# Transposes of a convolution's columns moved from the matmul engine to DMA, in a hybrid decoder block on one Trainium2 core

## The chip, the cores and the metric

The kernel runs on one core of one Trainium2 chip. The metric is the device time of the core in microseconds (us), the median of three runs. One further execution was taken with the hardware profiler, and all rows below come from it. The engines are PE (TensorE, matmuls; its weight loads are listed as PEld), DVE (VectorE), ACT (ScalarE), POOL (GpSimd) and SP (SyncE, which here only issues DMA transfers).

## What is computed

One layer of a decoder block on x of 256 tokens by 2048, all in float32:

```
hn = RMSNorm(h)
[q | k | v | z | xBC | dt | gate] = hn @ w_in
attention: per head, RMSNorm of q and k, ALiBi, causal (256 tokens are one MoBA block)
ssm: xBC = silu(causal depthwise conv over 4 tokens of xBC + bias)
     xs, B, C = split(xBC)              # 4096, 1024, 1024 columns
     y = chunked SSD scan(xs, dt, a, B, C), chunks of 128 tokens, 8 groups
     y = (y + d_skip * xs) * silu(z), RMSNorm per group of 512 columns, times norm_w
h += (sigmoid(g1) * (attn @ w_attn_out) + sigmoid(g2) * (y @ w_ssm_out)) @ w_out
h += relu(RMSNorm(h) @ w_up)^2 @ w_down
```

The projection xBC has 6144 columns: B and C (2048) are wanted with channels on the partitions, xs (4096) with tokens on the partitions. The convolution runs over tokens, so it is done with channels on the partitions, where a shift by a token is a shift in the free dimension.

## The kernel before

All large products go through one stream of **blocks**, numbered 0 to 87. A block is 512 columns of one weight matrix times 2048 rows, in 8 **units** of two 128-row tiles. SP loads a unit into one of four raw slots (`load_block`, L366), ACT rounds it to whi (L849), DVE takes the rest, wlo = raw - whi (L1268), and PE does three matmuls per tile and token half: xh*whi, xh*wlo, xl*whi (L485 to L487), 12 per unit and 96 per block, into two PSUM banks of a set (`stream`, L469). ACT and DVE work `LEAD` = 3 units ahead of PE: in step s of a block their program has the split of unit s+3 and then the other work put at step s (`steps`, L851 and L1271). There is no scheduler: every engine runs its program in the written order, and a wait holds up all that is behind it on that engine. SP loads a unit once the split four units earlier has freed the slot (L369).

Blocks 12 to 23 (`B_CONV` = 12) are the projection xBC: conv blocks m = 0 to 3 are B and C, m = 4 to 11 are xs. Conv block m is projected in block 12+m and convolved during block 13+m:

- ACT evacuates the PSUM set at step 7, scaled, to c_st (`conv_evac`, L1021).
- PE turns c_st into channel-major form in 8 transposes of 128x128 in float32, a matmul with the identity (`conv_T`, L645, recorded at L454), after unit 1, into PSUM banks 4 and 5.
- ACT makes the first tap with the bias from PSUM (`conv_first`, L1030), DVE adds three taps for each of four column tiles (`conv_taps`, L1451, 12 operations), ACT applies silu (`conv_silu`, L1043).
- For m of 4 and up, PE turns the result back in 8 transposes (`conv_back`, L662) after unit 6, and ACT copies it to xs (`conv_out`, L1049).

Conv block 11 has both of its transposes and all its taps in block 24, the first block of the SSD phase (`B_SSD` = 24). The common order of an SSD block is: PE does the product C*B (`seg`, L720) after unit 1 and the y product (`ssd_y`, L703, 8 products recorded at L710) after unit 4; DVE makes M, the decay matrix, in `ssd_seg` at step 0 (L1495, L1498), ACT takes its exponential (`ssd_exp`, L1080) at step 2, DVE multiplies it (`ssd_M`, L1515) at step 3. In block 24 these stand later: seg after unit 5, y after unit 7. POOL sets up the parameters of the next conv block (`conv_par`, L1802) once the taps of the last are done, and then the operands of the SSD groups (`ssd`, L1816): BTg, CTg, xd, xf.

The MLP's blocks already turn a tile by DMA: ACT splits r_st into its two 16-bit planes (`r_halve`, L1224), SP issues one `dma_start_transpose` per plane (`r_turn`, L359), and DVE joins the planes (`f_join`, L1676).

Of the kernel before, what the change touches and what calls it, by code (L numbers as in the profile page):

```python
# [22 lines left out]
D = 2048  # L23
T = 256
# [37 lines left out]
def build(nc, x, mix_norm_w, w_in, q_norm_w, k_norm_w, conv_w, conv_b, dt_bias, a_log, d_skip, ssm_norm_w,  # L62
# [13 lines left out]
    with ctx:  # L76
# [48 lines left out]
        c_st = [sb(f"c_st{i}", "E", 4 * KB * i, [P, NTOK, COLS]) for i in range(2)]  # L125
        cacc = sb("cacc", "E", 8 * KB, [P, 4, T])
        cT = sb("cT", "E", 12 * KB, [P, 4, T])
# [145 lines left out]

        c_T = sem("c_T")
# [83 lines left out]
        def _(sp):  # L358
# [7 lines left out]
            def load_block(b, w, row0, col0, turn=None):  # L366

                for s in range(SLOTS if isinstance(b, int) and b == 0 else 0, US):
# [4 lines left out]
                    if turn is not None and s >= US - 2:  # L373
                        r_turn(turn, s - US + 2)

# [22 lines left out]
            with sp.Fori(0, 4) as m:  # L398
                load_block(B_CONV + m, w_in, 0, XBC0 + INNER + m * COLS)
            with sp.Fori(0, 8) as m:  # L400
                load_block(B_CONV + 4 + m, w_in, 0, XBC0 + m * COLS)
# [10 lines left out]
            def ssd_loads(j1):  # L412
                load_rows(4 * j1 - 4, 2 * j1 - 2, 0)
                load_block(B_SSD + 4 * j1 - 4, w_in, 0, Z0 + 2 * j1 * COLS - 2 * COLS)
                load_rows(4 * j1 - 3, 2 * j1 - 2, 1)
                load_block(B_SSD + 4 * j1 - 3, w_in, 0, GATE0 + j1 * COLS - COLS)
# [33 lines left out]
        def _(pe):  # L450
# [194 lines left out]
            def conv_T(m, i, staged, backs):  # L645

                def f():
                    pe.wait_ge(set_free[i], staged)
                    if later(m):
                        pe.wait_ge(c_silu, m)  # L650
                        if later(backs):
                            pe.wait_ge(c_out, backs)
                    else:
                        pe.wait_ge(set_free[2], 4)
                    for c in range(4):
                        for t in range(NTOK):
                            o = (c % 2) * T + t * P
                            last = transpose(ps[4 + c // 2][:, o:o + P], c_st[i][:, t, c * P:(c + 1) * P])
                    last.then_inc(c_T, 1)
                return f  # L660

            def conv_back(m, src):  # L662
                def f():
                    pe.wait_ge(c_silu, m + 1)
                    for t in range(NTOK):
                        for c in range(4):
                            last = transpose(ps[4 + t][:, c * P:(c + 1) * P], src[:, c, t * P:(t + 1) * P])
                    last.then_inc(c_back, 1)
                return f

            a = attention(3)

            def conv_after(m, i, staged, backs, src=None, more=None):
                d = dict(more or {})
                d[1] = d.get(1, []) + [conv_T(m, i, staged, backs)]
                if src is not None:
                    d[6] = d.get(6, []) + [conv_back(m, src)]
                return d

# [3 lines left out]
            stream(B_CONV + 1, 1, 4, xT_hi, xT_lo, after=conv_after(0, 0, 5, 0, more=a[1]))  # L683
            stream(B_CONV + 2, 0, 5, xT_hi, xT_lo, after=conv_after(1, 1, 5, 0, more=a[2]))
            stream(B_CONV + 3, 1, 5, xT_hi, xT_lo, after=conv_after(2, 0, 6, 0))
            stream(B_CONV + 4, 0, 6, xT_hi, xT_lo, after=conv_after(3, 1, 6, 0))
# [3 lines left out]
            stream(B_CONV + 11, 1, 9, xT_hi, xT_lo, after=conv_after(10, 0, 10, 6, cT))  # L690
# [24 lines left out]
            def ssd_after(n, c, g):  # L715
# [9 lines left out]
                def banks_free():  # L725
                    pe.wait_ge(c_out, 8)
# [112 lines left out]
        def _(act):  # L839
# [181 lines left out]
            def conv_evac(m, k, i):  # L1021
                def f():
                    block_done(B_CONV + m)
                    if not (isinstance(m, int) and m < 2):
                        act.wait_ge(c_T, m - 1)
                    A(c_st[i][:, 0, :], SETS[k][0][:, :], ACT.Copy, scale=rstd1[:, 0:1])
                    A(c_st[i][:, 1, :], SETS[k][1][:, :], ACT.Copy, scale=rstd1[:, 1:2]).then_inc(set_free[k], 1)
                return f

            def conv_first(m):  # L1030
                def f():
                    act.wait_ge(c_T, m + 1)
                    act.wait_ge(c_par, m + 1)
                    if later(m):
                        act.wait_ge(c_silu, m)
                    for c in range(4):
                        i = A(cacc[:, c, :], ps[4 + c // 2][:, (c % 2) * T:(c % 2 + 1) * T], ACT.Identity,
                              scale=cw[:, 3, c:c + 1], bias=cb[:, c:c + 1])
                        if c % 2:
                            i.then_inc(c_first, 1)  # L1040
# [8 lines left out]
            def conv_out(m):  # L1049
# [855 lines left out]
```

## Time and profile before

| | |
|---|---|
| three runs | 2054.35, 2055.06, 2055.19 us, median 2055.06 |
| the profiled execution | 2054.75 us, its span 2052.7 us |
| granted TensorE clock | 1.0 of full speed over the whole span |
| busy, share of the span | PE 99%, PEld 83%, DVE 59%, ACT 51%, POOL 9% |
| DMA | 394 MB, 192 GB/s |

The span runs from the first to the last record of the core; the 2.05 us beside it are start and end. Conv blocks 12 to 23 lie at about 309 to 590 us, the SSD blocks 24 to 39 at 590 to 985 us, the MLP from 1353 us. "Busy" for PE means that some matmul was in flight: matmuls of 0.39 us start every 0.227 us. A bracket at the end of a timeline row gives the idle time of the engine before it and what ended it.

### The profile page before, as it was taken

To read this page: it belongs to the slowest core of one execution; us is meant where nothing else is said; L and a number is where in the kernel's file an instruction comes from. 1 tells how busy PE (TensorE), PEld (TensorE's weight loads), DVE (VectorE), ACT (ScalarE), POOL (GpSimd) and SP (SyncE) were. 2 spreads that over 40 slices of the span, in tenths; PEclk is the share of its full clock that TensorE was granted. 3 is DMA by queue.
4 is the path that set the end of the run, shared out by engine and by line. 5 is a ranking of instruction groups with operands and counts; after the bars stand their busy time and mean duration, and the time that the engine had idled before them with its cause. 6 is when DMAs were issued, how large, how long until landed. Compare 5 with 4: busy or idle time off the path is not lost.

```text
span 2052.7 us, 27154 instructions
## 1 busy us (share of the span) xinstructions
PE 2041.6 (99%) x9374; PEld 1694.7 (83%) x9374; DVE 1216.3 (59%) x1346; ACT 1037.7 (51%) x1238; POOL 189.4 (9%) x210
## 2 busy tenths in 40 slices
PE   9999999999999999999999999999999999999999
PEld 8888888888888888888888888888888888888887
DVE  5665566666666666666655555555545555554654
ACT  6454555555565454545554444455435534534542
POOL 2110010000012111111210000000000000000000
PEclk9999999999999999999999999999999999999999
DMA  7656555656665655666555556567667666666765
GB/s 241 186 164 183 166 167 171 178 176 179 178 201 177 194 194 184 196 198 190 174 183 185 193 187 225 194 185 223 203 193 211 213 193 202 204 210 194 201 218 163
DMA packets 231213, 394.08 MB, mean 192 GB/s; under 512 B 45776, under 2 KB 46736, under 8 KB 230880
## 3 DMA queue, kind: packets, MB, share of 16 engines
q1 hardware_dynamic: 229712, 389.54, 62.0%
q10 hardware_dynamic: 960, 2.75, 0.4%
q0 software_dynamic: 464, 0.77, 0.2%
q8 instruction: 47, 0.77, 0.2%
q14 instruction: 30, 0.25, 0.0%
HBM read 382.46 MB, written 2.16 MB: 187 GB/s over the span
## 4 chain that ended last, share of the span: by engine, by line
PE 97%; DVE 1%; ACT 1%; issue 0%; DMA 0%; DVEq 0%; ACTq 0%
PE ps L485 31%; PE ps L487 31%; PE ps L486 30%; PE ps L454 2%; PE ps L710 1%; ACT whi L849 0%; PE ps L562 0%; PE ps L539 0%; PE ps L699 0%; DVE f_st L1682 0%; DVE fT_lo L1690 0%; PE ps L720 0%; DVE cacc L1462 0%; ACT fT_hi L1236 0%; DVE wlo L1268 0%
## 5 line engine op out<-in xcount | busy, mean ns | idle before, releaser
L1268 DVE TENSOR_TENSOR wlo<-raw,whi 128x1024 fp32r<-128x1024 f32 x703 | 892.2, 1277 | 669.1 <-ACT whi L849 667.4
L849 ACT ACTIVATE whi<-raw 128x1024 fp32r<-128x1024 f32 x703 | 736.5, 1058 | 645.5 <-PE ps L487 628.6
L485 PE MATMUL ps<-whi,xT_hi 128*128 128x512 f32 x1276 | 509.5, 399 | 0.0
L487 PE MATMUL ps<-whi,xT_lo 128*128 128x512 f32 x1276 | 498.1, 390 | 0.0
L486 PE MATMUL ps<-wlo,xT_hi 128*128 128x512 f32 x1276 | 496.9, 389 | 0.0
L487 PEld LDWEIGHTS ps<-whi,xT_lo 128*128 128x128 f32 x1276 | 239.5, 188 | 51.3
L486 PEld LDWEIGHTS ps<-wlo,xT_hi 128*128 128x128 f32 x1276 | 240.0, 188 | 47.8 <-issue 1.0
L485 PEld LDWEIGHTS ps<-whi,xT_hi 128*128 128x128 f32 x1276 | 239.8, 188 | 47.8 <-issue 1.3
L485 PE MATMUL ps<-whi,fT_hi 128*128 128x512 f32 x512 | 199.6, 390 | 3.3 <-DVE fT_lo L1690 3.3
L485 PE MATMUL ps<-whi,hT_hi 128*128 128x512 f32 x512 | 199.3, 389 | 0.0
L487 PE MATMUL ps<-whi,fT_lo 128*128 128x512 f32 x512 | 199.2, 389 | 0.0
L486 PE MATMUL ps<-wlo,fT_hi 128*128 128x512 f32 x512 | 199.2, 389 | 0.0
L487 PE MATMUL ps<-whi,hT_lo 128*128 128x512 f32 x512 | 199.2, 389 | 0.0
L486 PE MATMUL ps<-wlo,hT_hi 128*128 128x512 f32 x512 | 199.2, 389 | 0.0
L485 PEld LDWEIGHTS ps<-whi,fT_hi 128*128 128x128 f32 x512 | 96.1, 188 | 24.8 <-ACT whi L849 3.8
L486 PEld LDWEIGHTS ps<-wlo,hT_hi 128*128 128x128 f32 x512 | 96.1, 188 | 20.0
L487 PEld LDWEIGHTS ps<-whi,hT_lo 128*128 128x128 f32 x512 | 96.1, 188 | 19.9
L487 PEld LDWEIGHTS ps<-whi,fT_lo 128*128 128x128 f32 x512 | 96.1, 188 | 19.9
L486 PEld LDWEIGHTS ps<-wlo,fT_hi 128*128 128x128 f32 x512 | 96.1, 188 | 19.9
L485 PEld LDWEIGHTS ps<-whi,hT_hi 128*128 128x128 f32 x512 | 96.1, 188 | 19.8
L485 PE MATMUL ps<-whi,sT_hi 128*128 128x512 f32 x256 | 99.9, 390 | 0.0
L487 PE MATMUL ps<-whi,sT_lo 128*128 128x512 f32 x256 | 99.6, 389 | 0.0
(254 smaller groups left out, 1856.7 us busy)
## 6 DMA issues: line engine op xcount, KB each, us to landing
raw<-in_w_in SPq DMA_DIRECT2D x319, 512.0 KB, 3.8
raw<-in_w_up SPq DMA_DIRECT2D x128, 512.0 KB, 4.1
raw<-in_w_down SPq DMA_DIRECT2D x128, 512.0 KB, 4.3
raw<-in_w_ssm_out SPq DMA_DIRECT2D x64, 512.0 KB, 4.2
raw<-in_w_attn_out SPq DMA_DIRECT2D x32, 512.0 KB, 4.3
raw<-in_w_out SPq DMA_DIRECT2D x32, 512.0 KB, 4.4
arow<-arows SPq DMA_DIRECT2D x16, 512.0 KB, 4.9
h<-in_x ACTq DMA_DIRECT2D x1, 2048.0 KB, 12.0
```

Source lines behind the costliest of these rows:

```text
L454: return nc.tensor.transpose(dst, src, ident[:, :])
L485: mm(dst, xh, whi[sl][:, kk, :], start=(s == 0 and kk == 0), stop=False)
L486: mm(dst, xh, wlo[sl][:, kk, :], start=False, stop=False)
L487: last = mm(dst, xl, whi[sl][:, kk, :], start=False, stop=(s == US - 1 and kk == UK - 1))
L710: last = mm(ps[6][:, hh * SHD:(hh + 1) * SHD], M[:, hh, :], xf[:, hh, :], start=True, stop=True)
L849: A(whi[s % SLOTS][:, :, :], raw[s % SLOTS][:, :, :], ACT.Copy).then_inc(hi_ready, 1)
L1268: V.tensor_tensor(wlo[s % SLOTS][:, :, :], raw[s % SLOTS][:, :, :], fp(whi[s % SLOTS][:, :, :]), ALU.subtract).then_inc(lo_ready, 1)
```

## The change

1. Conv blocks 0 to 10 are turned to channel-major form by DMA. ACT, which evacuates as before, splits c_st into two 16-bit planes (`c_halve`, step 0), SP turns each plane by a DMA transpose (`c_turn`: the first after the load of unit 7 of the block, the second after unit 0 of the next; SP runs about 7 units ahead of PE), and DVE joins them to cx (`c_join`, step 3). The taps read cx in SBUF instead of PSUM.
2. For m = 4 to 10 the result goes back the same way: `x_halve` on ACT (step 2 of the next block), `x_turn` on SP (after units 2 and 3), `x_join` on DVE (step 7), straight into xs.
3. Conv block 11 keeps PE's transposes, in block 24, where the SSD work takes its common place, and the taps stand around it.
4. The convolution works one half block later than before: first tap at step 4, taps at steps 5 and 6, silu at step 1 of the next block.
5. c_st has one buffer instead of two. SP's conv loop and DVE's loops are written out or shortened; POOL waits for two groups of xs before its SSD work instead of one.

```diff
+            def c_turn(m, a):
+                sp.wait_ge(c_halved, m + 1)
+                if m:
+                    sp.wait_ge(c_joined, m)
+                sp.dma_start_transpose(c_tiles[:, a, :, :], c_half[:, a, :, :].rearrange("p t n -> p (t n)")) \
+                    .then_inc(c_turned, 16)
+            def x_turn(m, a):
+                sp.wait_ge(x_halved, m - 3)
+                if m > 4:
+                    sp.wait_ge(c_out, m - 4)
...
+            def conv_turns(j, s):
+                if s == 0 and 2 <= j <= 12:
+                    c_turn(j - 2, 1)
+                if s in (2, 3) and 7 <= j <= 13:
+                    x_turn(j - 3, s - 2)
+                if s == 7 and 1 <= j <= 11:
+                    c_turn(j - 1, 0)
...
-            stream(B_CONV + 1, 1, 4, xT_hi, xT_lo, after=conv_after(0, 0, 5, 0, more=a[1]))
...
-            with pe.Fori(0, 3) as i:
-                stream(B_CONV + 5 + 2 * i, 1, 6 + i, xT_hi, xT_lo, after=conv_after(4 + 2 * i, 0, 7 + i, 2 * i, cT))
-                stream(B_CONV + 6 + 2 * i, 0, 7 + i, xT_hi, xT_lo, after=conv_after(5 + 2 * i, 1, 7 + i, 1 + 2 * i, cT))
+            stream(B_CONV + 1, 1, 4, xT_hi, xT_lo, after=a[1])
...
+            with pe.Fori(0, 4) as i:
+                stream(B_CONV + 4 + 2 * i, 0, 6 + i, xT_hi, xT_lo)
+                stream(B_CONV + 5 + 2 * i, 1, 6 + i, xT_hi, xT_lo)
...
-                return {0: [conv_T(11, 1, 10, 7)], 3: [conv_back(11, cT)], 5: [banks_free, seg],
-                        7: [ssd_y(n, c, g)]}
+                return {0: [conv_T], 1: [banks_free, seg], 4: [ssd_y(n, c, g)], 7: [conv_back]}
...
+            def c_halve(m, k, staged):
+                def f():
+                    act.wait_ge(set_free[k], staged)
+                    if later(m):
+                        act.wait_ge(c_turned, 32 * m)
+                    A(c_half[:, :, :, :].rearrange("p a t n -> p a (t n)"),
+                      halves(c_st[:, :, :].rearrange("p t n -> p (t n)")), ACT.Copy).then_inc(c_halved, 1)
...
+            def conv_work(j, k, staged, more=None):
                 d = dict(more or {})
+                add(d, 0, c_halve(j - 1, 1 - k, staged))
...
+                    add(d, 1, conv_silu(j - 2, dst))
+                    if not (isinstance(j, int) and j < 6):
+                        add(d, 2, x_halve(j - 2))
+                add(d, 4, conv_first(j - 1))
+                add(d, 7, conv_evac(j, k))
...
-                    steps(b, {1: [conv_first(11)], 3: [conv_silu(11, cT[:, :, :])], 4: [conv_out(11)],
-                              6: [ssd_exp(n)], 7: [z_sigmoid(b, g)]})
+                    steps(b, {1: [ssd_exp(n), conv_silu(10, cacc[:, :, :])], 2: [x_halve(10)], 3: [conv_first(11)],
+                              6: [conv_silu(11, cacc[:, :, :])], 7: [conv_out, z_sigmoid(b, g)]})
...
+            def c_join(m):
+                def f():
+                    dve.wait_ge(c_turned, 32 * m + 32)
+                    if later(m):
+                        dve.wait_ge(c_tap, 12 * m)
+                    for a in range(2):
+                        i = V.tensor_copy(halves(cx[:, :, :].rearrange("p c t -> p (c t)"))[:, a, :],
+                                          c_tiles[:, a, :, :].rearrange("p (t c) l -> p c t l", t=NTOK))
...
+            def conv_work(j, more=None):
                 d = dict(more or {})
+                add(d, 3, c_join(j - 1))
+                add(d, 5, conv_taps(j - 1, 0))
+                add(d, 6, conv_taps(j - 1, 1))
+                if not (isinstance(j, int) and j < 6):
+                    add(d, 7, x_join(j - 2))
...
-                    steps(b, {0: [ssd_seg(n, 0, g)], 1: [conv_taps(11, 0, 0), conv_taps(11, 0, 1)],
-                              2: [conv_taps(11, 1, 0), conv_taps(11, 1, 1)],
-                              6: [ssd_cbm(n, 0, g)], 7: [ssd_M(n), z_gate(g), ssd_y(n, 0, g)]})
+                    steps(b, {0: [ssd_seg(n, 0, g)], 1: [ssd_cbm(n, 0, g)], 3: [ssd_M(n)], 4: [conv_taps(11, 0)],
+                              5: [ssd_y(n, 0, g), conv_taps(11, 1)], 7: [z_gate(g)]})
...
-            pool.wait_ge(c_out, 1)
+            pool.wait_ge(c_out, 2)
```

On PE, in block 23 (conv block 11 is projected, 10 convolved), the end of unit 1 before:

```order
L487 MATMUL ps<-whi_54,xT_lo 128x512
L454 MATMUL ps<-ident,c_st_91 128x128 [waits c_out,c_silu,set_free0]
L454 MATMUL ps<-ident,c_st_91 128x128 x7
L485 MATMUL ps<-whi_55,xT_hi 128x512 [waits lo_ready,hi_ready]
```

Such a group, and one of cT after unit 6, is gone from each block of the loop and from this one. The c_st group that is left stands in block 24, after unit 0; now:

```order
L520 MATMUL ps<-whi_53,xT_lo 128x512
L487 MATMUL ps<-ident,c_st 128x128 [waits set_free2,set_free1]
L487 MATMUL ps<-ident,c_st 128x128 x7
L518 MATMUL ps<-whi_54,xT_hi 128x512 [waits lo_ready,hi_ready]
```

On ACT, from the split of unit 6 to M's exponential in block 24 before (L849 is the weight split, M the decay matrix):

```order
L849 ACTIVATE whi_55<-raw_51 128x1024 [waits unit_used,raw_in2]
L1046 ACTIVATE cT<-cacc 128x1024 [waits c_tap]
L849 ACTIVATE whi_56<-raw_52 128x1024 [waits unit_used,raw_in3]
L1053 ACTIVATE xs<-ps 128x512 [waits c_back]
L1054 ACTIVATE xs<-ps 128x512
L849 ACTIVATE whi_53<-raw_49 128x1024 [waits unit_used,raw_in0]
L849 ACTIVATE whi_54<-raw_50 128x1024 [waits unit_used,raw_in1]
L1083 ACT_TABLE_LOAD
L1083 ACTIVATE M<-M 128x1024 [waits seg_done]
```

and now, from the split of unit 4 to that of unit 6 and the first tap behind it (L860 is the weight split):

```order
L860 ACTIVATE whi_53<-raw_49 128x1024 [waits unit_used,raw_in0]
L1116 ACT_TABLE_LOAD
L1116 ACTIVATE M<-M 128x1024 [waits seg_done]
L1073 ACT_TABLE_LOAD
L1073 ACTIVATE cacc<-cacc 128x1024 [waits c_tap]
L860 ACTIVATE whi_54<-raw_50 128x1024 [waits unit_used,raw_in1]
L1081 ACTIVATE x_half<-cacc 128x2048 [waits x_turned,c_silu]
L860 ACTIVATE whi_55<-raw_51 128x1024 [waits unit_used,raw_in2]
L1065 ACTIVATE cacc<-ps,cb,cw 128x256 [waits c_silu,x_halved,c_par,c_T]
```

M's exponential moved from between the splits of units 9 and 10 to just behind that of unit 4, and silu and x_halve of conv block 10 stand between it and the splits of units 5 and 6.

On DVE, around M's product in block 24 now (L1303 is the weight split, L1569 the product that y waits for):

```order
L1303 TENSOR_TENSOR wlo_58<-raw_50,whi_54 128x1024 [waits hi_ready]
L1303 TENSOR_TENSOR wlo_59<-raw_51,whi_55 128x1024 [waits hi_ready]
L1569 TENSOR_TENSOR M<-M,cbm 128x1024 [waits dec_done,cbm_done]
L1303 TENSOR_TENSOR wlo_60<-raw_52,whi_56 128x1024 [waits hi_ready]
L1510 SCALAR_TENSOR_TENSOR cacc<-ps,cw,cacc 128x255 [waits c_first]
```

Before, all taps of conv block 11 stood ahead of that product; now it stands behind the split of unit 6 alone, and they behind it.

## Rows read from the trace of the kernel before

**Rows 1.** The page: span, busy time, chain of waits, the weight split of ACT, raw's landing.

```profile
span 2052.7 us, 27154 instructions
...
PE 2041.6 (99%) x9374; PEld 1694.7 (83%) x9374; DVE 1216.3 (59%) x1346; ACT 1037.7 (51%) x1238; POOL 189.4 (9%) x210
...
PE 97%; DVE 1%; ACT 1%; issue 0%; DMA 0%; DVEq 0%; ACTq 0%
...
L849 ACT ACTIVATE whi<-raw 128x1024 fp32r<-128x1024 f32 x703 | 736.5, 1058 | 645.5 <-PE ps L487 628.6
...
raw<-in_w_in SPq DMA_DIRECT2D x319, 512.0 KB, 3.8
```

**Rows 2.** PE's groups by line: matmul or transpose, busy us, mean ns, idle before.

```profile
L485 PE MATMUL ps<-whi,fT_hi 128*128 128x512 f32 x512 | 199.6, 390 | 3.3 <-DVE fT_lo L1690 3.3
...
L454 PE MATMUL ps<-ident,c_st 128*128 128x128 f32 x96 | 12.4, 272 | 0.0
...
L454 PE MATMUL ps<-ident,cT 128*128 128x128 f32 x64 | 8.4, 274 | 1.7 <-ACT cT L1046 1.7
```

**Rows 3.** The chain in order of time: start us, us, what.

```profile
454.30 0.88 PE ps L454 x8
...
572.20 0.87 PE ps L454 x8
...
1628.10 0.47 PE ps L485
...
1803.33 0.47 PE ps L485
```

**Rows 4.** Timeline of PE in block 24: start us, us, instruction [idle <- releaser].

```profile
590.18 0.39 PE L485 MATMUL ps<-whi,xT_hi 128*128 128x512 f32 x1
...
603.80 1.09 PE L454 MATMUL ps<-ident,cT 128*128 128x128 f32 x8 [1.69 <-ACT cT L1046]
...
617.31 2.00 PE L710 MATMUL ps<-xf,M 128*128 128x64 f32 x16 [1.01 <-DVE M L1515]
619.11 0.48 PE L485 MATMUL ps<-whi,xT_hi 128*128 128x512 f32 x1
```

**Rows 5.** The MLP's turned tile f_half: its transfers, its copies, landing times.

```profile
L363 SPq DMA_TRANSPOSE f_half<-r_half x32: 1237/1237/1827, 1375.8 to 1968.6; - x32
L1682 DVE COPY f_st<-f_half x32: 739/747/756, 1384.2 to 1975.2; 128x1024 uint16<-128x1024 uint16 x32
...
DMA to landing us min/median/max: 3.0/3.9/5.1
```

**Rows 6.** The MLP's staged planes r_half: ACT's split into halves.

```profile
L1229 ACT ACTIVATE r_half<-r_st x16: 1912/1912/1912, 1373.8 to 1964.7; 128x2048 uint16<-128x2048 uint16 x16
```

**Rows 7.** Windows of one block: without turns, then with two (PEclk, DMA share, GB/s last).

```profile
1358.20:1380.00 21.80, 21.80 (x98) 18.06 (x97) 11.86 (x12) 12.06 (x12) 3.51 (x2) 1.00 0.59 164
1380.00:1402.00 22.00, 22.00 (x99) 18.23 (x98) 13.14 (x12) 12.17 (x12) 1.90 (x1) 1.00 0.75 227
```

**Rows 8.** Timeline of ACT: first tap of a conv block, a table load in block 24.

```profile
455.21 1.93 ACT L1037 ACTIVATE cacc<-ps,cb,cw 128x256 f32<-128x256 f32 x4 [2.54 <-PE ps L454]
...
611.55 1.28 ACT L1083 ACT_TABLE_LOAD   x1
```

**Rows 9.** Timeline of DVE: six taps, a weight split beside POOL, the two segment operations.

```profile
461.96 2.42 DVE L1462 SCALAR_TENSOR_TENSOR cacc<-ps,cw,cacc 128x255 f32<-128x255 f32 x6
...
585.62 2.06 DVE L1268 TENSOR_TENSOR wlo<-raw,whi 128x1024 fp32r<-128x1024 f32 x1
...
593.77 1.22 DVE L1495 TENSOR_TENSOR M<-arow,acum 128x1024 f32<-128x1024 f32 x1
595.02 0.70 DVE L1498 TENSOR_SCALAR M<-M 128x1024 f32<-128x1024 f32 x1
```

**Rows 10.** Timeline of POOL from the last tap of conv block 10 to xd.

```profile
582.46 1.00 POOL L1805 COPY cb<-par 128x4 f32 x1 [22.09 <-DVE cacc L1462]
...
584.58 2.02 POOL L1825 TENSOR_TENSOR xd<-xs,dtd 128x512 f32<-128x512 f32 x1
```

More of the change, by code:

```diff
@@ L124, in build @@
         x_in = sb("x_in", "E", 0, [P, NTOK, D])
-        c_st = [sb(f"c_st{i}", "E", 4 * KB * i, [P, NTOK, COLS]) for i in range(2)]
-        cacc = sb("cacc", "E", 8 * KB, [P, 4, T])
-        cT = sb("cT", "E", 12 * KB, [P, 4, T])
+        c_st = sb("c_st", "E", 0, [P, NTOK, COLS])
+        c_half = sb("c_half", "E", 4 * KB, [P, 2, NTOK, COLS], u16)
+        cx = sb("cx", "E", 8 * KB, [P, 4, T])
+        cacc = sb("cacc", "E", 12 * KB, [P, 4, T])
+        c_tiles = sb("c_tiles", "W", 0, [P, 2, NTOK * 4, P], u16)
+        x_half = sb("x_half", "W", 4 * KB, [P, 2, 4, T], u16)
+        x_tiles = sb("x_tiles", "D", 16 * KB, [P, 2, 4 * NTOK, P], u16)
         merged = sb("merged", "E", 0, [P, NTOK, D])
@@ L374, in load_block @@
                         r_turn(turn, s - US + 2)
+                    if conv is not None:
+                        conv_turns(conv, s)
             sp.dma_start(prow[0:KT, 3, :], mix_norm_w[0].rearrange("(a b) -> a b", b=P)).then_inc(mix_loaded, 16)
@@ L397, in _ @@
                 load_block(B_QKV + 3 * g + 2, w_in, 0, V0 + g * COLS)
[L398 to L401, printed above, removed]
+            for m in range(12):
+                load_block(B_CONV + m, w_in, 0, XBC0 + (INNER + m * COLS if m < 4 else (m - 4) * COLS), conv=m)
             def load_rows(n, g, c):
@@ L642, in _, with conv_T, conv_back @@
                 qkv_group(g)
[L645 to L654, printed above, removed]
-                    for c in range(4):
[L656 to L669, printed above, removed]
-            a = attention(3)
[L673 to L678, printed above, removed]
+            def conv_T():
+                pe.wait_ge(set_free[1], 10)
+                pe.wait_ge(set_free[2], 4)
+                for c in range(4):
+                    for t in range(NTOK):
+                        o = (c % 2) * T + t * P
+                        last = transpose(ps[4 + c // 2][:, o:o + P], c_st[:, t, c * P:(c + 1) * P])
+                last.then_inc(c_T, 1)
+            def conv_back():
+                pe.wait_ge(c_silu, 12)
+                for t in range(NTOK):
+                    for c in range(4):
+                        last = transpose(ps[4 + t][:, c * P:(c + 1) * P], cacc[:, c, t * P:(t + 1) * P])
+                last.then_inc(c_back, 1)
+            a = attention(3)
             pe.wait_ge(qkT_ready, 7)
@@ L1031, in f @@
                 def f():
-                    act.wait_ge(c_T, m + 1)
+                    if isinstance(m, int) and m == 11:
+                        act.wait_ge(c_T, 1)
+                    else:
+                        act.wait_ge(c_joined, m + 1)
                     act.wait_ge(c_par, m + 1)
@@ L1476, in _ @@
             steps(B_CONV, a[0])
-            steps(B_CONV + 1, conv_work(0, a[1]))
-            steps(B_CONV + 2, conv_work(1, a[2]))
-            steps(B_CONV + 3, conv_work(2))
-            steps(B_CONV + 4, conv_work(3))
-            with dve.Fori(0, 3) as i:
-                steps(B_CONV + 5 + 2 * i, conv_work(4 + 2 * i))
-                steps(B_CONV + 6 + 2 * i, conv_work(5 + 2 * i))
-            steps(B_CONV + 11, conv_work(10))
+            for j in range(1, 6):
+                steps(B_CONV + j, conv_work(j, a[j] if j < 3 else None))
+            with dve.Fori(0, 6) as i:
+                steps(B_CONV + 6 + i, conv_work(6 + i))
             def xs_at(g, t):
```

119 lines of the change are left out of this document (69 added, 50 removed).

## The prediction

> **What bounds the kernel now.** I read the page first. PE is busy for 99% of the span and the chain of waits lies on it for 97%, so the time is the length of PE's own program plus its few waits. ACT's weight split idles 645.5 us, 628.6 of them behind PE [rows 1]: ACT and DVE wait for PE. So an instruction taken out of PE's program is worth its full length, and work added to ACT, DVE or SP costs nothing until it makes PE wait. PE's groups by line say where it does: almost no idle time beside any of them, 3.3 us in all before the MLP's down products, 1.7 before the cT transposes [rows 2].
>
> The chain in order of time gives the price of what goes. From the c_st transposes of block 18 to those of block 23 are five blocks in 117.90 us, 23.58 each, with two groups of 8 transposes in each. The first matmuls of two down blocks, 8 blocks apart, are 175.23 us apart; one wait of 3.3/4 = 0.83 us lies between, felt as about 1.0 since matmuls overlap by 0.16. That leaves (175.23 - 1.0)/8 = 21.78 for a block without transposes [rows 2, 3]. So a group costs (23.58 - 21.78)/2 = 0.90 us of PE; the chain itself gives it 0.87 to 0.88 [rows 3].
>
> **The first SSD block.** Block 24 lasts from 590.18 to 619.11 us and has two waits in it: 1.69 us before the cT transposes and 1.01 us before the y product [rows 4]. Each delays the next start by 0.16 more, so 3.0 us in all.
>
> **What the change removes.** Of 96 c_st transposes 88 go, of 64 cT transposes 56 [rows 2]; the order of PE's instructions shows one group of each left. These are 18 groups: 18 x 0.90 = **-16.2 us**, or -15.8 at the chain's price. All of it is on the path. On ACT seven copies of xs go too, worth nothing, for ACT has idle time.
>
> **What it adds in the conv blocks.** Three things per turned tile, all priced by the MLP, which does the same at the same shape: ACT's split into planes, 1.91 us [rows 6], two transfers that hold SP 1.24 us each and land in 3.0 to 5.1 us, median 3.9, and a join of two copies, 0.75 us each [rows 5], 1.4 together. From conv block 4 on there are two such tiles per block.
>
> ACT then does, per block of 21.8 us: 8 splits of 1.06 [rows 1], evacuation 1.3 (an estimate, two copies of half the size of a split), two plane splits 3.8, first tap 1.93 [rows 8], silu about as long as a split: 16.6 us. DVE: 8 splits of 1.22 (the size of M's row), 12 taps in two runs of 2.42 [rows 9], four copies 3.0: 17.6 us. Both fit. The order fits as well. With t = 0 at the start of a block, ACT has the planes at 4.3, SP issues the two turns at about 5.5 and 7.4 (after the loads of unit 7 and of unit 0), and the second lands at 11.3, by the longest landing at 12.5. DVE gets to the join behind the split of unit 6, at 11.2. So it waits up to 1.3 us there, with all its splits behind it; but that split of unit 7 is wanted only at 7 x 2.72 = 19.1 and is done by 15. The last split of the block, behind the taps, ends near 24.3 and is wanted at 27.2. I cost these blocks at nothing: the cover is the lead of three units, 8.2 us, of which some 5 are eaten at the worst place. Behind the join ACT's first tap waits, and ACT's split of the next block's unit 0 behind that, ready at 15.7 and wanted at 21.8. The attention steps in blocks 13 and 14 stand on DVE in between; by the same walk the last head's normalisation, which PE's transposes wait for, is done just as PE comes: 0.1 us, 0 to 0.5.
>
> DMA: a block with two turns shows a share of 0.75 and 227 GB/s, the one before without turns 0.59 and 164 [rows 7]. Two more add as much again: 0.59 + 0.32 = 0.91 in blocks 18 to 23, which have four. It is close to full, but a weight load that lands in 3.8 us [rows 1] is issued some 8 us before ACT wants it. Cost nothing; upper bound in a rival.
>
> At this place the Trainium skill speaks against the change. Its page "VectorE: DVE Perf Modes", in "The three transpose paths" and the rules below it, gives a 128x128 16-bit transpose by DMA as 1309 ns and by TensorE as 390 ns, and advises TensorE where PSUM will do. By that figure one plane of 8 tiles would take 10.5 us if its tiles ran one after the other, four planes 42 us of a 21.8 us block, and the sum would be slower than before. The trace does not bear that out: 8 tiles land in 3.9 us [rows 5], and 8 float32 transposes hold PE for 0.90. What matters here is whose time it is.
>
> **What it does to block 24.** PE wants y after unit 4 now: 5 x 2.72 + 0.9 for the c_st group + 0.2 for seg = 14.7 us. The y product waits for M, and M goes through this queue. DVE ends the previous block late, behind taps and x_join, at about 4.0; split of unit 3 until 5.2; the segment pair 1.22 + 0.70 [rows 9] until 7.1. POOL's parameter copies and SSD operands now start with the last tap of conv block 10, which has moved into block 24: xd starts 2.1 us behind it [rows 10], at 3.8, just there. A POOL operation beside DVE makes a 1.22 us DVE operation 2.06 [rows 9]: one to two such hits, 0.8 to 1.7, I take 1.2. So the segments are ready at 8.3. ACT: exponential 1.0 (9.3), table load 1.28 [rows 8] for silu (10.6), silu (11.5), split of unit 5 (12.5), x_halve 1.9 (14.4), split of unit 6 (15.4). DVE: split of unit 6 (16.5), M's product 1.2 (17.7). **PE waits 3.0 us**, between 1.5 (no hits, DVE on time) and 4.5 (late turns as well). The back transposes after unit 7 find silu done, at 26.9 against 27.8. So the two old waits, 3.0 us, go, and one of about the same size takes their place. Block 25 starts with DVE five microseconds behind, as the silu of block 11, its copy and a table load stand ahead of the z gate; the same walk gives M 0.4 us late there, 0 to 1.5.
>
> **The sum.** 2054.75 - 16.2 - 3.0 + 3.0 + 0.4 + 0.1 = 2039.05 for the profiled execution. The median of the three runs is 0.3 above it, so I forecast **2039.3 us**, 15.8 below 2055.06.
>
> **The rivals.**
>
> *Block 24 runs smoothly*: no wait takes the place of the old ones, since the turns land early and the POOL hits are small. For it: the exponential now stands four splits earlier. Against: three ACT operations and a table load before the split of unit 6. 2055.06 - 16.2 - 3.0 = 2035.9.
>
> *The conv blocks pay*: joins come late by more than the lead covers, at c_join behind the second turn. For it: a DMA share of 0.9 in the last six conv blocks, and the MLP's SP turn is issued with nothing else in flight. If each of 11 blocks loses 0.3 to 0.6 us, 3 to 7 us come back: 2042.6 to 2046, middle 2044.
>
> *DMA becomes the bound*, the case that ends slower: place, the weight loads of blocks 18 to 23, with four turns each. Two turns took 0.16 of 21.8 us, that is 1.7 us of all engines each. If beside loads each takes double, the share is 0.59 + 0.64 = 1.23 and each block gets 0.23 x 21.8 = 5 us longer: 2055.06 - 16.2 + 6 x 5 = 2069. It decides from 16.2/6 = 2.7 us lost per block. Against: the MLP's blocks with two turns have no wait at all. The skill's figure above would lead here.
>
> *The change does not do what it says*: excluded for the most part, for PE's order of instructions shows the 18 groups gone; a turned tile that waited for PE would be all that is left of it.
>
> **How the numbers follow.** The forecast's own case has 0.60, with 2037.4 to 2042.3 from the bounds 1.5 to 4.5, 0 to 1.5 and 0 to 0.5; block 24 smooth 0.17; conv blocks pay 0.18; DMA the bound 0.04; nothing happens 0.01. The range 2035.2 to 2044.0 takes in the first two and half of the third. About 0.2%, 4 us, is what a measurement of this kernel tells from no change. Faster by more than that is all but the last two cases, 0.95; same 0.01; slower 0.04.
>
> **What would show it.** In the profile after: 8 transposes from c_st and 8 from cacc; conv blocks of 21.8 us from 385 us on with no idle time in front of their matmuls; in block 24 one idle of 2 to 4 us before the y product, ended by M, and none before the cacc transposes; turns landing in 4 to 5 us; the DMA share near 0.9 in the last conv blocks. I am wrong if PE waits for wlo in a conv block (then the lead was too short), if block 24 shows no wait (then DVE was earlier or POOL did not hit), or if loads end ACT's idle time there.

## The result, and the profile after

Ten runs of the changed kernel have a median of **2059.86 us** (2057.87 to 2062.83); ten of the kernel before, on the same chip, 2055.48 (2054.35 to 2056.58). The ratio is 1.0022, 95% interval 1.0013 to 1.0031: slower by 0.2%, where 15.8 us less were forecast. The prediction was wrong by 20.6 us, and its range ended 16 us short.

The page of the changed kernel, against [rows 1]:

```profile
span 2056.8 us, 26718 instructions
...
PE 2033.2 (99%) x9230; PEld 1681.2 (82%) x9230; DVE 1236.0 (60%) x1382; ACT 1065.3 (52%) x1243; POOL 231.1 (11%) x210
...
PE 88%; DVE 4%; issue 3%; DMA 3%; ACT 2%; SPq 1%; POOL 0%; DVEq 0%; ACTq 0%; POOLq 0%
...
L860 ACT ACTIVATE whi<-raw 128x1024 fp32r<-128x1024 f32 x703 | 736.2, 1058 | 645.0 <-PE ps L520 598.4
L518 PE MATMUL ps<-whi,xT_hi 128*128 128x512 f32 x1276 | 510.6, 400 | 8.8 <-DVE wlo L1303 8.7
```

PE has 144 instructions fewer and 8.4 us less busy time, and the chain of waits lies on it for 88% of the span instead of 97%. The 9% that left it are the story: DVE 4%, DMA 3%, ACT 2% and issue 3% now stand in the chain, so these engines have stopped being covered. The view of PE's waits names two new ones (columns: total us, number, longest):

```profile
PE ps L518 <- DVE wlo L1303: 8.7, 16, 1.9
PE ps L733 <- POOL CTg L1876: 5.6, 1, 5.6
```

Neither was in the prediction, and neither is the wait for M that was. The first lies in the convolution blocks. The windows there (PEclk, DMA share and GB/s last), against [rows 7]:

```profile
309.00:385.00 76.00, 76.00 (x350) 63.11 (x350) 50.96 (x83) 50.29 (x71) 5.41 (x10) 1.00 0.67 183
408.00:432.00 24.00, 23.54 (x104) 19.17 (x103) 15.34 (x22) 14.02 (x16) 4.88 (x5) 1.00 0.79 198
504.00:528.00 24.00, 22.77 (x98) 17.94 (x97) 16.67 (x24) 15.37 (x17) 6.17 (x5) 1.00 0.92 211
575.00:598.00 23.00, 18.06 (x76) 14.21 (x74) 14.56 (x23) 10.02 (x13) 4.85 (x3) 0.93 0.86 215
598.00:630.00 32.00, 29.54 (x133) 24.60 (x134) 20.39 (x29) 21.51 (x24) 8.36 (x10) 0.89 0.59 163
```

PE is idle from the stretch 408:432 on, where a block has only two turns, and at a DMA share of 0.79. DVE is busy for only 16.7 of 24 us in 504:528 and still late. Its timeline shows why: ten of the eleven joins now wait for their turn. Here is one round of it, with SP's DMA issues of the same round below:

```profile
497.08 1.39 DVE L1518 COPY xs<-x_tiles 128x1024 uint16 x2
508.14 1.40 DVE L1492 COPY cx<-c_tiles 128x1024 uint16<-128x1024 uint16 x2 [5.01 <-DMA c_tiles<-c_half]
512.71 1.23 DVE L1303 TENSOR_TENSOR wlo<-raw,whi 128x1024 fp32r<-128x1024 f32 x1 [2.07 <-ACT whi L860]
513.86 2.45 DVE L1510 SCALAR_TENSOR_TENSOR cacc<-cx,cw,cacc 128x255 f32<-128x255 f32 x6
520.86 1.40 DVE L1518 COPY xs<-x_tiles 128x1024 uint16 x2
```

```profile
500.07 1.24 SPq L380 DMA_TRANSPOSE c_tiles<-c_half  x1
501.35 0.58 SPq L404 DMA_DIRECT2D raw<-in_w_in  x1
502.03 1.53 SPq L380 DMA_TRANSPOSE c_tiles<-c_half  x1
...
523.85 1.24 SPq L380 DMA_TRANSPOSE c_tiles<-c_half  x1
```

Read them as a loop. DVE joins at 508.14 and reaches the x join at 520.86. Behind it come the splits of units that let go the load of unit 7 and, behind that load, the first turn (523.85, 23.78 us after the one of 500.07); then the load of unit 0, then the second turn, which from 502.03 takes 6.1 us to land; then the next join. It runs 12.7 us from join to x join and 11.1 from x join to join, **23.8 us round, where a block of PE is 21.8**. From the block at 390 us on, the joins are 22.8 to 23.9 us apart, the last one 26.0. DVE's join copies idle 41.0 us in 10 waits before them. The turned tile lands later than the MLP's [rows 5], and holds SP longer:

```profile
L380 SPq DMA_TRANSPOSE c_tiles<-c_half x22: 1237/1452/3309, 335.4 to 573.7; - x22
...
  DMA c_tiles<-c_half: 41.0, 10
...
DMA to landing us min/median/max: 3.5/5.6/7.5
```

The second new wait is in block 24: C x B waits for POOL's copy CTg, which stands behind the copy of the last block's biases and taps. Where [rows 10] has 1.00 us for the bias copy there are 4.52 now, and 2.04 for the taps:

```profile
593.15 4.52 POOL L1859 COPY cb<-par 128x4 f32 x1 [18.84 <-DVE cacc L1510]
597.61 2.04 POOL L1861 COPY cw<-par 128x4 f32 x4
599.59 0.39 POOL L1875 COPY BTg<-BT 128x256 f32<-128x256 f32 x1
599.92 0.40 POOL L1876 COPY CTg<-CT 128x256 f32<-128x256 f32 x1
```

```profile
600.47 1.19 PE L733 MATMUL ps<-CTg,BTg 128*128 128x256 f32 x2 [5.55 <-POOL CTg L1876]
601.10 0.99 PE L518 MATMUL ps<-whi,xT_hi 128*128 128x512 f32 x1
601.88 0.63 PE L519 MATMUL ps<-wlo,xT_hi 128*128 128x512 f32 x1
602.31 0.63 PE L520 MATMUL ps<-whi,xT_lo 128*128 128x512 f32 x1
```

A third loss hangs on these waits: the clock. Matmuls start 0.43 us apart (601.88, 602.31) instead of 0.23, half the granted clock (the level of 1.2 GHz instead of 2.4), for some 9 matmuls after this wait of 5.55 us and for 8 after the one of 1.85 us at 583.95. The last two windows above show the same as a mean granted clock of 0.93 and 0.89.

The account, from the starts of PE's matmuls: the wlo waits delay starts by 11.3 us in all (8.7 idle, and 0.16 more each), and the matmul behind such a wait is followed after 0.31 us instead of 0.23, 1.1 us over the 16 of them. C x B adds 5.7, the half clock 3.7, together 21.8. Against 16.2 + 3.0 us saved that makes +2.6; the stretch from 309 us to the start of block 25 measures 313.3 us against 310.2, so 0.5 us are in no item of mine. The spans differ by 1.0 us more, and nearly all of it comes in the MLP: two idles at 1702 and 1878 us, which the profile puts down to issue, delay starts by 0.4 to 0.5 us each.

### The profile page after: what moved, and what is told of

It is laid out like the page before. It is cut to its first block, busy times and chain, and to the rows that moved or that the text cites. A ratio compares the mean times of both kernels' runs of the same rounds, so it can differ in the third digit from the quotient of the medians.

```text
span 2056.8 us, 26718 instructions
## 1 busy us (share of the span) xinstructions
PE 2033.2 (99%) x9230; PEld 1681.2 (82%) x9230; DVE 1236.0 (60%) x1382; ACT 1065.3 (52%) x1243; POOL 231.1 (11%) x210
## 3 DMA queue, kind: packets, MB, share of 16 engines
q8 instruction: 63, 1.03, 0.2%
## 4 chain that ended last, share of the span: by engine, by line
PE 88%; DVE 4%; issue 3%; DMA 3%; ACT 2%; SPq 1%; POOL 0%; DVEq 0%; ACTq 0%; POOLq 0%
PE ps L518 28%; PE ps L520 28%; PE ps L519 28%; DMA c_tiles<-c_half 2%; PE ps L487 2%; DVE wlo L1303 1%; PE ps L723 1%; DVE cacc L1510 1%; ACT whi L860 1%; ACT cacc L1065 1%; PE ps L572 0%; PE ps L595 0%; DVE xs L1518 0%; PE ps L712 0%; SPq L380 0%
## 5 line engine op out<-in xcount | busy, mean ns | idle before, releaser
L1303 DVE TENSOR_TENSOR wlo<-raw,whi 128x1024 fp32r<-128x1024 f32 x703 | 891.0, 1276 | 631.7 <-ACT whi L860 629.6
L860 ACT ACTIVATE whi<-raw 128x1024 fp32r<-128x1024 f32 x703 | 736.2, 1058 | 645.0 <-PE ps L520 598.4
```

Source lines behind the costliest of these rows:

```text
L860: A(whi[s % SLOTS][:, :, :], raw[s % SLOTS][:, :, :], ACT.Copy).then_inc(hi_ready, 1)
L1303: V.tensor_tensor(wlo[s % SLOTS][:, :, :], raw[s % SLOTS][:, :, :], fp(whi[s % SLOTS][:, :, :]), ALU.subtract).then_inc(lo_ready, 1)
```

## The experiments

Two theories for the convolution blocks. **The loop**: the turn stands in a circle of waits that is longer than a block. **Crowding**: the DMA engines, at 0.9, make turns and loads late. For block 24: **POOL's copies** hold C x B, or something else would hold PE there anyway.

**Both turns one load earlier** (e1_turns_early).

```diff
-                if s == 0 and 2 <= j <= 12:
-                    c_turn(j - 2, 1)
-                if s == 7 and 1 <= j <= 11:
-                    c_turn(j - 1, 0)
+                if s in (6, 7) and 1 <= j <= 11:
+                    c_turn(j - 1, s - 6)
```

> The changed kernel with both turns of a c tile issued one place earlier: the first after the load of unit 6, the second after that of unit 7, as the MLP has them. Theory A (a ring: the split of unit 3 on DVE frees SP's load of unit 7, the turns stand behind it, the join behind their landing, first tap, taps and x_join behind that, and the next split of unit 3 behind those; the ring takes 23.8 us in a block of 21.8): the turns start some 2 us earlier in the ring, the period of the conv blocks falls to 22 us or less, most of the 12 us of waits for wlo go, the time is 2048 to 2051 us. Theory B (bandwidth: DMA share 0.9, the turns and loads can't go faster in any order): the period stays 23.8 us, the time 2059 to 2060 us.

Measured: 2042.34 us (2039.30 to 2043.62), ratio 0.9934 (0.9920 to 0.9947). That is more than either theory had said. The turn of the columns, from its tile's view, and PE's waits:

```profile
L380 SPq DMA_TRANSPOSE c_tiles<-c_half x22: 1231/1237/1890, 336.1 to 558.9; - x22
...
  DMA c_tiles<-c_half: 2.9, 7
...
DMA to landing us min/median/max: 3.1/4.4/5.4
```

```profile
PE ps L731 <- POOL CTg L1874: 3.7, 1, 3.7
```

DVE's wait fell from 41.0 to 2.9 us and no wlo wait is left; the wait for CTg is shorter too, 3.7 us where it was 5.6. The same bytes go through engines that are as full:

```profile
480.00:504.00 24.00, 24.00 (x108) 19.87 (x107) 17.75 (x25) 17.39 (x20) 3.89 (x5) 1.00 0.99 250
```

A share of 0.99 and PE without a pause: crowding does not set the time here.

**The join one step later** (e2_join_late), the other end of the same loop.

```diff
-                add(d, 4, conv_first(j - 1))
+                add(d, 5, conv_first(j - 1))
...
-                add(d, 3, c_join(j - 1))
+                add(d, 4, c_join(j - 1))
```

> The changed kernel with c_join behind the split of unit 7 instead of unit 6, and the first tap behind ACT's next split. Theory A (the ring): join to taps no longer holds a split on ACT and one on DVE, the ring is 1 to 2 us shorter and the split of unit 7 no longer waits, time 2049 to 2054 us. Theory B (bandwidth): 2059 to 2060 us.

Measured: 2041.55 us (2040.72 to 2043.68), ratio 0.9934 (0.9921 to 0.9948), again more than the 2049 to 2054 us that I had expected of the loop. The landing is 4.9 us in the median and up to 7.8, and DVE waits for it once, 1.4 us. One more split of a unit stands in the time that DVE had spent waiting, and the way from join to x join is 9.7 us (499.96 to 509.68) where it was 12.7.

**Only the first turn earlier, only the second** (e10_first_turn_early, e11_second_turn_early). In the first, `s == 7` becomes `s == 6` for `c_turn(j - 1, 0)`; in the second:

```diff
-                if s == 0 and 2 <= j <= 12:
-                    c_turn(j - 2, 1)
...
                 if s == 7 and 1 <= j <= 11:
                     c_turn(j - 1, 0)
+                    c_turn(j - 1, 1)
```

> The change with only the first of a convolution block's two column turns issued one load earlier (after the load of unit 6), the second where the change has it (after the load of unit 0 of the next block). With both a load earlier all waits of the convolution blocks went. Theory A, a loop: join, taps, VectorE's splits, the load that a split lets go, the turn behind that load, its landing, the next join; it ran 23.8 us round where a block is 21.8, and a turn that is one load (2.7 us) earlier shortens it only if it is the one that lands last. Moving the first alone shortens nothing: 2057 to 2061 us. Rival, that the two turns ran close together and crowded each other or the loads: spreading them gives part of the 18 us back: 2045 to 2054 us.

> The change with only the second turn issued earlier: right behind the first, after the load of unit 7, so ahead of the load of unit 0 instead of behind it. Theory A, the loop through the turn that lands last: it is shortened by the load that the turn no longer stands behind (its issue 0.6 us, and its 512 KB ahead of it in the DMA engines, 0.6 to 2 us): between 0.6 and 2.6 of the 2.0 us per block that the loop is too long, so 2043 to 2056 us, and SP's turn-to-join time shrinks by as much. Rival, crowding: two turns back to back land later, and nothing is won: 2057 to 2062 us.

Measured: 2054.75 us (2051.36 to 2056.42), ratio 0.9995 (0.9986 to 1.0005), and 2042.06 (2041.70 to 2043.21), ratio 0.9934 (0.9917 to 0.9950). The second turn is what counts, as the loop has it. The first is worth more than the nothing that I had said: 2054.75 lies between the range of the loop and that of its rival. The second came out just below its range, and against its rival: back to back the turns land in 4.5 us in the median, not later than the 5.6 of the change. DVE's rows of the two, the first turn earlier above:

```profile
495.31 1.39 DVE L1518 COPY xs<-x_tiles 128x1024 uint16 x2
505.31 1.38 DVE L1492 COPY cx<-c_tiles 128x1024 uint16<-128x1024 uint16 x2 [3.53 <-DMA c_tiles<-c_half]
518.01 1.40 DVE L1518 COPY xs<-x_tiles 128x1024 uint16 x2
```

```profile
488.99 1.41 DVE L1517 COPY xs<-x_tiles 128x1024 uint16 x2
497.96 1.41 DVE L1491 COPY cx<-c_tiles 128x1024 uint16<-128x1024 uint16 x2
510.69 1.40 DVE L1517 COPY xs<-x_tiles 128x1024 uint16 x2
```

From join to x join it is 12.7 us in these two as in the change. From x join to join it was 11.1 with the change, is 10.0 with the first turn gone from in front of the second (that its 1.24 us on SP are part of the loop, which I had overlooked, would explain it), and 9.0 with the second turn ahead of a load. So 23.8, 22.7 and 21.7 us round. In the last the join does not wait, so that DVE goes at PE's pace of 21.8 there; the rows show that the loop is no longer than a block, not how much shorter it is.

**The change without the x turns** (e4_no_x_turns). For groups 0 to 5 VectorE's copy reads ScalarE's planes and waits for them instead of the transposes, and 12 of the 14 transposes are not issued:

```diff
-                if s in (2, 3) and 7 <= j <= 13:
+                if s in (2, 3) and j == 13:
...
-                            x_tiles[:, a, :, :].rearrange("p (c t) l -> p t c l", t=NTOK))
+                            (x_tiles[:, a, :, :] if isinstance(m, int) and m == 10 else
+                             x_half[:, a, :, :].rearrange("p c (t l) -> p (c t) l", l=P))
+                            .rearrange("p (c t) l -> p t c l", t=NTOK))
...
```

> The change without 12 of the 14 transposes that turn the x part back: VectorE's copy reads ScalarE's planes directly, so that the x of six groups of heads stays unturned and the outputs that follow from it are not the reference's; the work of every engine is as in the change, and only the queue and the DMA engines have less. Theory A (the place of the turns in the ring of loads): the turn of the columns still stands between the load of unit 7 and the join, so waits for it stay; with less traffic it lands nearer to the 3.9 us of the early blocks than to 6, and 2 to 5 of the 11.5 us of late starts go: 2054 to 2058 us. Theory B (crowded DMA engines make the landing late, and the x turns are what crowds them): the waits in the blocks that turn x back go nearly all, those of the two blocks before stay, and it is 2046 to 2051 us.

Measured: 2060.48 us (2058.76 to 2062.14), ratio 1.0027 (1.0015 to 1.0039). The window at 504 us has a share of 0.75 (0.92 before the edit), and PE's and DVE's busy times are nearly the same:

```profile
504.00:528.00 24.00, 22.62 (x98) 17.78 (x97) 16.61 (x24) 15.91 (x18) 7.17 (x5) 1.00 0.75 196
```

```profile
  DMA c_tiles<-c_half: 41.7, 10
...
DMA to landing us min/median/max: 3.3/5.6/7.6
```

Crowding by the x turns falls: nearly a fifth of the DMA engines' busy time less, the same waits for the turn, the same landing of 5.6 us. The time is above both ranges: I had expected 2 to 5 us from a quicker landing, and it did not become quicker. What makes 5.6 us of 3.9 is not the x turns. The loads that SP issues around the turn remain: with the second turn ahead of one of them (e11_second_turn_early) the median is 4.5 us. A kernel with fewer loads was not tried.

**The last block's biases and taps in tiles of their own** (e3_own_par), so that POOL copies them early and CTg stands behind nothing.

```diff
+        cw2 = small("cw2", [P, 4, 4])
+        cb2 = small("cb2", [P, 4])
...
-            with pool.Fori(0, 8) as m:
+            with pool.Fori(0, 7) as m:
                 conv_par(4 + m, m)
+            conv_par(11, 7, cb2, cw2)
...
```

> The changed kernel with tap weights and bias of conv block 11 in tiles of their own, so that POOL copies them a block earlier and has BTg and CTg ready long before block 24. Theory P (PE's wait of 5.55 us before the product C*B is POOL's late copies, held up for 4.5 us behind DVE): the wait goes, and with it the stretch at the lower clock after it, 6 to 8 us in all: 2052 to 2054 us. Rival (something else, the segments on DVE, holds block 24 as long): y waits instead, 2057 us or more. The conv blocks stay as they are.

Measured: 2060.04 us (2058.40 to 2062.27), ratio 1.0024 (1.0014 to 1.0035): nothing is won, as the rival had it. PE came to C x B on time, and stood at the next point for M:

```profile
PE ps L520 <- DVE wlo L1306: 7.5, 15, 1.5
PE ps L725 <- DVE M L1573: 5.3, 1, 5.3
```

This is the wait that the prediction had for block 24. In the changed kernel it was hidden behind the one for CTg.

**The order of block 24 alone**, in the kernel before with all its transposes (e5_ssd_order_alone).

```diff
-                return {0: [conv_T(11, 1, 10, 7)], 3: [conv_back(11, cT)], 5: [banks_free, seg],
-                        7: [ssd_y(n, c, g)]}
+                return {0: [conv_T(11, 1, 10, 7)], 1: [banks_free, seg], 4: [ssd_y(n, c, g)], 7: [conv_back(11, cT)]}
...
```

The rest of the edit gives ACT and DVE the order of the change in this block: M's exponential at step 1, M x cbm at step 3, the taps at steps 4 and 5.

> The kernel before with part 3 of the change alone: block 24 in the common order, conv block 11's taps around it, all transposes on PE. Its two waits of block 24 (3.0 us) stand where they were before. If the order itself is good, both go and nothing comes: 2052.5 us. If M is late behind ACT's queue as I had predicted, a wait of 1 to 3 us before y takes their place: 2054 to 2055.5 us. A wait for POOL as in the changed kernel is not expected, since the taps of conv block 10 end in block 23.

Measured: 2052.08 us (2051.29 to 2052.38), ratio 0.9984 (0.9975 to 0.9993): 3.0 us, all of the two old waits, and no new one, as expected. POOL's bias copy takes 1.00 us there and the four tap copies 0.55. So neither the late CTg nor the late M comes from the new order alone. Late turns are part of it, but not all: with convolution blocks that run without a wait, 3.7, 2.8 and 3.0 us of the wait for CTg are left (e1_turns_early, e2_join_late, e11_second_turn_early). These kernels have the later convolution and this one has not: the last taps, the x join and the silu of conv block 10 fall into the time of block 24 there. That was not tested apart.

**All of it together.** Four kernels combine the edits. e6_all has both turns earlier, the join later and the tiles of their own; e7_late_own the join later with the tiles of their own; e8_late_own_M adds M x cbm one step earlier in block 24; e9_early_own_M is e8_late_own_M with the turns earlier instead of the join later.

```diff
-                    steps(b, {0: [ssd_seg(n, 0, g)], 1: [ssd_cbm(n, 0, g)], 3: [ssd_M(n)], 4: [conv_taps(11, 0)],
+                    steps(b, {0: [ssd_seg(n, 0, g)], 1: [ssd_cbm(n, 0, g)], 2: [ssd_M(n)], 4: [conv_taps(11, 0)],
```

> The change with both turns of a convolution block issued after the loads of units 6 and 7, with VectorE's join and ScalarE's first tap one step later, and with the last block's biases and taps in tiles of their own, copied early by POOL. With the turns earlier, or the join later, alone, every wait of the convolution blocks went, and what stayed in block 24 was TensorE's wait of 2.8 to 3.7 us for POOL's copy CTg, behind copies of 4.5 and 2.0 us, and some 14 matmuls at half clock after it (2 to 3 us). Theory A: POOL's copies were the last obstacle, and with them out of block 24 the sum is that of the prediction without its new wait: 2054.8 - 16.2 - 3.0 = 2035.6, so 2035 to 2038 us. Theory B: as in the kernel with the own tiles alone, where TensorE came on time to C*B and then stood 5.3 us before the next step for M, the wait for M takes the place of the wait for CTg: then 2040 to 2043 us, as with the turns earlier alone.

> As the kernel with all three edits, but the turns where the change has them: only the join and the first tap one step later, and the last block's biases and taps in tiles of their own. Theory A (slack for the turn, wherever it comes from, and POOL's copies out of the way): the same time as with all three, 2035 to 2038 us. Rival: the turn of a block landed up to 7.8 us after its issue with the join later alone, against 5.4 at most with the turns earlier, so here a wait or two for the turn stays, each worth 1 to 2 us: 2037 to 2041 us.

> The kernel with the join a step later and the last block's tiles of their own, and in block 24 VectorE's M x cbm at step 2 instead of 3, so ahead of one wlo that waits for ScalarE. In the kernel without this M x cbm started at 588.98 us behind a wlo of 587.83 us (1.15 us), and TensorE stood 1.33 us for it. Theory A: the wait goes with the step: M is ready 2.7 to 3.9 us earlier, and the time is 1 to 2 us under the 2040.5 us of that kernel: 2038 to 2040 us (profiled span 2035.5 to 2036.5). Rival: M is late for ScalarE's exponential, not for the wlo: then M x cbm starts no earlier, wlo is held up behind it, and it is 2040 to 2042 us.

> The change with both turns of a block issued after the loads of units 6 and 7 (join and first tap where the change has them), the last block's biases and taps in tiles of their own, and M x cbm at step 2 of block 24. Theory A: all three delays that the change brought are gone (turn, POOL's copies, M), so the sum is 2054.8 - 16.2 - 3.0 = 2035.6: profiled span 2033.5 to 2036, median 2036 to 2039. Rival: with the join at step 3 VectorE is behind at block 24's start and a wait for C*B or M of 1 to 3 us stays: 2039 to 2042 us.

| kernel | median us (range) | ratio to before (95%) | profiled: span, wait in block 24 |
|---|---|---|---|
| e6_all | 2044.16 (2040.39 to 2044.39) | 0.9943 (0.9930 to 0.9957) | 2038.3, M 2.0 |
| e7_late_own | 2040.50 (2038.62 to 2041.61) | 0.9927 (0.9913 to 0.9940) | 2037.4, M 1.3 |
| e8_late_own_M | 2038.66 (2035.92 to 2041.70) | 0.9922 (0.9909 to 0.9936) | 2034.0, none |
| e9_early_own_M | 2040.83 (2038.38 to 2042.64) | 0.9929 (0.9916 to 0.9943) | 2038.8, silu 1.6 |

With POOL's copies out of the way PE waits for M in the first two, 1.3 to 2.0 us. The rows of the kernel with the join later show what M stood behind:

```profile
587.83 1.23 DVE L1306 TENSOR_TENSOR wlo<-raw,whi 128x1024 fp32r<-128x1024 f32 x1 [1.52 <-ACT whi L862]
588.98 1.22 DVE L1573 TENSOR_TENSOR M<-M,cbm 128x1024 f32<-128x1024 f32 x1
```

```profile
590.25 2.00 PE L725 MATMUL ps<-xf,M 128*128 128x64 f32 x16 [1.33 <-DVE M L1573]
```

One step earlier it is gone. The profiled run of e8_late_own_M, the fastest of its five, has no wait of PE in the blocks from 385 us to the MLP, its block 25 starts at 599.51 us against 622.27 with the change and 619.11 before [rows 4], and its time is 2035.92: that is 19.6 us less up to there, where 16.2 + 3.0 = 19.2 had been reckoned. It has the lowest median of all versions. Its runs spread over 5.8 us, though, where those of the order alone spread over 1.1. So the differences of a few us among these four, and from the 2041.55 us of the join one step later, are not shown by five runs each.

Of the forecasts, that for e8_late_own_M held; e7_late_own and e9_early_own_M came out in the ranges of their rivals, and e6_all, which has every edit but the last, above both of its ranges, which I can't explain. In e9_early_own_M the wait is neither of those that its rival names: PE stands 1.6 us before the back transposes, for ScalarE's silu.

Part of the spread lies outside the change. At two places of the MLP, near 1685 and 1860 us, PE has idles that the profile puts down to issue, where the kernel before and e8_late_own_M have none: 0.7 us in all in e6_all, 1.9 in e7_late_own, 3.1 in e9_early_own_M. With 1.6 us for silu, the 3.1 us make up nearly all of the 4.8 us between the spans of e9_early_own_M and e8_late_own_M; of the 3.4 us between e7_late_own and e8_late_own_M the wait for M is less than half. What these idles are stays open.

## Why the prediction was wrong

**The step that failed** is "I cost these blocks at nothing: the cover is the lead of three units, 8.2 us, of which some 5 are eaten at the worst place". It should have been +12.4 us (11.3 of late starts and 1.1 behind them), and it brought part of the half clock with it. Two things were wrong in it. The turn's landing was taken as 3.9 us, and here the median is 5.6. The 3.9 comes from a place in the MLP where SP has issued nothing for some 5 us before the first turn, as in the kernel before:

```profile
1392.02 0.37 SPq L371 DMA_DIRECT2D raw<-in_w_up  x1
1397.55 1.24 SPq L363 DMA_TRANSPOSE f_half<-r_half  x1
1398.83 0.58 SPq L371 DMA_DIRECT2D raw<-in_w_up  x1
1399.51 1.24 SPq L363 DMA_TRANSPOSE f_half<-r_half  x1
```

In the change two loads go out in the 2.78 us right before it (from 497.19 us). And the walk began each block anew at t = 0 with every engine on time. It found DVE waiting up to 1.3 us at the join and called that covered. But what DVE does late lets the next load go late, and with it the next turn: the walk should have gone once round, from join to join, and been compared with 21.8. The measured round with my landing (3.9 instead of 6.1) would be 23.8 - 2.2 = 21.6, on the edge; with the bound of 5.1 that I had, 22.8, and 1 us a block lost. The rival "the conv blocks pay", at a chance of 0.18, had the place right, joins late by more than the lead covers, and 3 to 7 us as its price; its 0.3 to 0.6 us a block should have been 1.1 over the eleven, and 2 in the last ones. Of its two reasons the DMA share was not the one that acted: 0.99 goes without a wait in e1_turns_early.

**Block 24.** The old two waits went: right, and shown by the order alone (3.0 us). The new wait for M: its mechanism was right, its size was not. It is 1.3 to 2.0 us in the kernels whose convolution blocks run smoothly (3.0 forecast, 1.5 as the lower bound), and 5.3 with late turns, for which I had 4.5 as the bound; in the changed kernel itself PE does not wait for M at all. What I had as "xd starts 2.1 us behind" the last tap was 7.1 us in the changed kernel (593.15 to 600.28), and so CTg, which I had not put on the path at all, stopped PE before M could.

**What was right.** The 18 groups at 0.90 us, with the 3.0 us of old waits, give 19.2; the best version measured 19.6 to the start of block 25. The DMA share of 0.91 (0.90 to 0.97 measured), and that DMA would not be the bound: PE runs through at 0.99, and 12 turns fewer change nothing. The times of ACT's and DVE's new work per block hold as well: 16.6 and 17.6 us forecast, 15.4 and 16.7 us busy in the 24 us of 504:528, which are a little more than one block. Block 25's 0.4 us and attention's 0.1 did not come: PE has no wait at either place in any of the profiles.

The Trainium skill, "VectorE: DVE Perf Modes", "The three transpose paths", spoke against the change with 1309 ns for a 128x128 transpose by DMA. The time came out longer, as its advice would have it, but for another reason: 8 tiles land in 5.6 us here, not in the 10.5 that the prediction had estimated from that figure, and a move by one step makes the change worth 13.6 us (2055.12 to 2041.55). What counted was a latency in a loop, not a rate.

## What to carry to other kernels

When a step of latency (a DMA turn) is put between two engines that also feed the main stream, go once round the circle of waits, through the queue that issues the transfer and every instruction ahead of it there, and compare the sum with the length of one iteration: below it the detour is free, above it every iteration pays the excess. Take the landing time from a place whose queue is as full as the new one, or use the longest seen, and put the transfer ahead of a load rather than behind it. When a wait goes, look which wait was hidden by it: in block 24 the one for M stood behind the one for CTg, and only the kernel without the first showed the second.

## What the hardware showed that I had not expected

**A small POOL copy beside a busy DVE.** The bias copy, 128x4, takes 1.00 us in the kernel before [rows 10] and 4.4 to 5.7 in the changed one from the copy at 426 us on, where DVE's splits, its 16-bit join copies and the segment operation follow each other without a pause. From 593.15 to 597.67 us DVE ran this:

```profile
592.89 1.22 DVE L1303 TENSOR_TENSOR wlo<-raw,whi 128x1024 fp32r<-128x1024 f32 x1
594.02 1.36 DVE L1518 COPY xs<-x_tiles 128x1024 uint16 x2
595.27 1.22 DVE L1303 TENSOR_TENSOR wlo<-raw,whi 128x1024 fp32r<-128x1024 f32 x1
596.40 1.23 DVE L1549 TENSOR_TENSOR M<-arow,acum 128x1024 f32<-128x1024 f32 x1
```

The copy lasts through five DVE instructions. The Trainium skill, "SBUF — State Buffer", "SBUF: two separate sides", says that VectorE and GpSimd share one pair of ports by an exclusive lock for a whole instruction: a VectorE operation in a 2-port mode, or one with two SBUF inputs, and a GpSimd one that reads SBUF shut each other out, whichever starts first. The trace fits a POOL that is shut out, but for several instructions in a row. The kernel with the join later shows what an unbroken row of DVE instructions does: at 443.59 us, with 1.03 us of idle time on DVE behind the split of 443.32, the bias copy takes 1.00 us; at 465.29 the x join fills that gap, and it takes 3.41. What lets the copy through in the end was not tried.

**The clock after a short wait.** A wait of 1.85 us was followed by 8 matmuls at half the granted clock (they begin with the fifth behind it) and one of 5.55 us by 9, 3.7 us in all with the C x B matmuls themselves: the clock took a sixth of what the change lost. After waits of 1.33 us (e7_late_own), 1.48 (e3_own_par), 1.68 (e4_no_x_turns) and 1.69 (the kernel before, [rows 4]) there is no such stretch. Nor does its length follow the wait: 11 matmuls after 3.67 us in e1_turns_early, 4 after 6.62 us in e4_no_x_turns. So a wait has no fixed price in clock here, and a forecast can only give it a range.
